# Expert outputs left in PSUM over all steps, x normalised in place, and gathers issued before the turns

## What is computed

```python
x = x + g1[:, None, :] * (merged @ w_out[i])
h = modulate(rms_norm(x, norm2_g[i]), sh2, sc2)
x = x + g2[:, None, :] * grouped_moe(h, router_w, router_bias, moe_w1[i], moe_w3[i], moe_w2[i])

# grouped_moe, t = the 256 tokens; gates = 0 for all but the 2 experts of a token
for e in range(N_EXPERTS):                       # 16 experts
    a = jax.nn.silu(t @ w1[e]) * (t @ w3[e])     # 1024 -> 512
    y = y + gates[:, e:e + 1] * (a @ w2[e])      # 512 -> 1024
```

## Time and profile before

| what | value |
|---|---|
| median of 3 runs | 1086.69 us (1086.66 to 1086.99) |
| profiled execution, span from first to last instruction | 1085.1 us |
| what lies around the span, against the median | 1.6 us |
| PE busy | 1046.2 us (96%), PEld 574.4, DVE 469.5, ACT 174.3 |
| HBM read | 330.54 MB, 306 GB/s over the span |
| chain that ended last | PE 82%, DMA 7%, DVE 6% |
| experts of layer 0, from gather(0) to the end of scatter(6) | 344.1 to 562.3 us |
| experts of layer 1, the same | 857.8 to 1073.4 us |
| PE busy between them, 562 to 857 us | 293.0 of 295 us |
| additions of scattered outputs to x (L1983) | 56, 688 ns each |
| TensorE's mean granted clock | 0.993 |

### The profile page before, as it was taken

How to read it: one execution, slowest core, us unless ns; L and a number is a source line. 1 busy time by engine, 2 the same in 40 slices (tenths; PEclk the granted TensorE clock), 3 DMA queues, 4 the chain that set the end, 5 groups by cost and what they waited for, 6 DMA issues and landing times.

```text
span 1085.1 us, 17591 instructions
## 1 busy us (share of the span) xinstructions
PE 1046.2 (96%) x7533; PEld 574.4 (53%) x7533; DVE 469.5 (43%) x1024; ACT 174.3 (16%) x340; POOL 20.4 (2%) x40
## 2 busy tenths in 40 slices
PE   7999999999999999999999999999999999999885
PEld 3688667654446344443448866765444634444322
DVE  3477696644125422352235769660112532222114
ACT  4021101310014113101121110031001410111102
POOL 3000000000000000000000000000000000000000
PEclk9999999999999999999999999999999999999998
DMA  9997846268953999999999884525665399999992
GB/s 305 391 386 256 304 157 214 79 216 321 413 229 135 411 420 415 421 421 420 421 398 368 295 301 166 185 89 194 252 266 217 137 422 421 420 421 421 421 420 118
DMA packets 90917, 332.78 MB, mean 307 GB/s; under 512 B 5020, under 2 KB 5355, under 8 KB 66005
## 3 DMA queue, kind: packets, MB, share of 16 engines
q1 hardware_dynamic: 87905, 323.56, 76.3%
q0 software_dynamic: 2048, 6.09, 1.6%
q10 hardware_dynamic: 884, 1.97, 0.6%
HBM read 330.54 MB, written 1.05 MB: 306 GB/s over the span
## 4 chain that ended last, share of the span: by engine, by line
PE 82%; DMA 7%; DVE 6%; SPq 3%; issue 1%; ACT 1%; DVEq 0%
PE bank L735 80%; DMA ring<-in_moe_w_dram 3%; SPq L665 2%; DMA wide<-in_moe_w_dram 2%; DMA ring<-in_w_ada_dram 2%; PE bank L1007 1%; PE bank L1175 1%; DVE wide L1586 0%; DVE area L1779 0%; DVE wide L1784 0%; DVE area L1782 0%; PE bank L1093 0%; DVE area L1781 0%; DVE area L1780 0%; PE bank L788 0%
## 5 line engine op out<-in xcount | busy, mean ns | idle before, releaser
L735 PE MATMUL bank<-ring,hT 128*32 128x512 f32 (+3 forms) x1808 | 311.6, 555 | 4.4 <-DMA ring<-in_moe_w_dram 1.8
L735 PE MATMUL bank<-hT,ring 128*32 128x256 f32 (+1 forms) x2112 | 214.1, 380 | 0.2 <-DVE hT L1620 0.2
L735 PEld LDWEIGHTS bank<-ring,hT 128*32 128x32 f32 (+2 forms) x1808 | 129.0, 136 | 152.8 <-issue 149.1
L735 PEld LDWEIGHTS bank<-hT,ring 128*32 128x32 f32 (+1 forms) x2112 | 158.7, 132 | 55.3 <-issue 8.7
L735 PE MATMUL bank<-area 32*64 32x64 f32 (+5 forms) x648 | 96.1, 363 | 0.5 <-ACT area L1468 0.5
L735 PE MATMUL bank<-ring,area 128*32 128x512 f32 x664 | 81.8, 594 | 0.5 <-ACT area L1468 0.5
L2051 DVE TENSOR_TENSOR area<-bank,area 128x512 f32<-128x512 f32 x14 | 9.7, 691 | 148.4 <-PE bank L735 148.4
L735 PEld LDWEIGHTS bank<-area 32*64 32x64 f32 (+4 forms) x648 | 43.8, 145 | 54.2 <-issue 52.2
L735 PE MATMUL bank<-wide,hT 128*32 128x512 f32 x368 | 65.9, 603 | 2.8 <-DMA ring<-in_moe_w_dram 1.4
L735 PE MATMUL bank<-ring,wide 128*128 128x512 f32 (+1 forms) x192 | 64.0, 597 | 0.8 <-DMA ring<-in_w_ada_dram 0.8
L1586 DVE SCALAR_TENSOR_TENSOR area<-ring,wide,area 128x512 f32<-128x512 f32 x84 | 63.1, 751 | 2.5
(11 more groups left out here) (266 smaller groups left out, 895.3 us busy)
## 6 DMA issues: line engine op xcount, KB each, us to landing
ring<-in_moe_w_dram SPq DMA_DIRECT2D x135, 1024.0 KB, 14.5
ring<-in_w_in_dram SPq DMA_DIRECT2D x26, 2048.0 KB, 11.4
ring<-in_w_ada_dram SPq DMA_DIRECT2D x24, 2048.0 KB, 14.2
wide<-in_moe_w_dram SPq DMA_DIRECT2D x33, 1024.0 KB, 12.2
cst<-in_moe_w_dram SPq DMA_DIRECT2D x13, 1024.0 KB, 14.9
area<-in_moe_w_dram SPq DMA_DIRECT2D x11, 1024.0 KB, 14.5
ring<-in_w_out_dram SPq DMA_DIRECT2D x4, 2048.0 KB, 8.0
ring<-in_w_br_h_dram SPq DMA_DIRECT2D x4, 1536.0 KB, 7.9
```

The costliest lines, as they stand in the source:

```text
L735: return pe.matmul(dst, lhsT, rhs, start=start, stop=stop, skip_group_check=True)
```

## The change

- The scattered outputs of all seven steps are summed in banks 2 to 5: only the first step's products start a sum. VectorE adds each bank to x once, after the last step (`add_experts`).
- x is normalised in place: x = x * rs. `root_x` holds the root of the mean square, so that `add_experts` writes x * root_x + bank, which gives the old x back.
- The gather reads x directly, with a step of 8 elements (`chunk_of`), since x isn't regrouped. It writes banks 6 and 7, as banks 2 to 5 are taken, and so does every filter piece.
- xn's memory is a further place for blocks, `NORMED`, free once the output product has read mT (`p_wo`).
- `gather(s + 1)` stands before the turn, with the filter pieces of spot 1 ahead of it; `scatter(s - 1)` stands between the two halves of the turn, and in the last step before `up(6, 1)`. `down(s)` waits until hg has been made from banks 6 and 7.

```diff
@@ place_blocks, SP
-                            + [f for f in free if f[0] < EXTRA] + [(EXTRA + 3, None)]
+                            + [f for f in free if f[0] < EXTRA] + [(NORMED, None), (EXTRA + 3, None)]
...
-            return bank[(5, 4 if L else 7)[n]]
+            return bank[(6 if L else 5, 7)[n]]
...
+                    elif u == NORMED:
+                        sp.wait_ge(p_wo, (L + 1) * 4)
@@ TensorE
+                def chunk_of(tt, k):
+                    return x[:, tt, :].rearrange("p (m k) -> p k m", k=ND)[:, k, :]
 
                 def gather(s):
                     pe.wait_ge(v_sel, L * STEPS + s + 1)
-                    if s >= 2:
-                        pe.wait_ge(v_acc, (L * STEPS + s - 2) * 4 + 2)
+                    if s:
+                        pe.wait_ge(v_yS, (L * STEPS + s - 1) * 2)
+                    if L + 1 < DEPTH and s == TAPS_STEP:
+                        pe.wait_ge(a_dec, (L + 2) * 8)
+                    if L + 1 < DEPTH and s - 1 == TAPS_STEP:
+                        pe.wait_ge(v_kt, (L + 1) * 12 + 8)
+                    if L + 1 < DEPTH and s - 1 == SPECTRA_STEP:
+                        pe.wait_ge(a_ks, (L + 2) * 8)
...
-                            last = mm(bank[2 + k // 4][:, (k % 4) * P:(k % 4 + 1) * P], xn[:, tt, k * P:(k + 1) * P],
+                            last = mm(bank[6 + k // 4][:, (k % 4) * P:(k % 4 + 1) * P], chunk_of(tt, k),
                                       sel[:, tt, :], tt == 0, tt == NT - 1)
...
                 def down(s):
                     n = L * STEPS + s
                     pe.wait_ge(a_actT, n + 1)
+                    if s < STEPS - 1:
+                        pe.wait_ge(a_hg, n + 2)
+                        pe.wait_ge(v_hg, n + 2)
...
                             mm(bank[2 + 2 * tt + h][:, :], selT[:, tt * P:(tt + 1) * P],
-                               yS[:, h * W:(h + 1) * W], True, True).then_inc(p_sc, 1)
+                               yS[:, h * W:(h + 1) * W], s == 0, s == STEPS - 1).then_inc(p_sc, 1)
...
                     up(s, 0)
                     next_filter(s, 0)
+                    if s == STEPS - 1:
+                        scatter(s - 1)
                     up(s, 1)
-                    if s:
-                        scatter(s - 1)
-                    turn(s)
+                    next_filter(s, 1)
                     if s < STEPS - 1:
                         gather(s + 1)
-                    next_filter(s, 1)
+                    turn_act(s)
+                    if 0 < s < STEPS - 1:
+                        scatter(s - 1)
+                    turn_sel(s)
                     down(s)
@@ ScalarE
-                    last = sc.activation(xn[:, tt, :].rearrange("p (k m) -> p k m", k=ND),
-                                         x[:, tt, :].rearrange("p (m k) -> p k m", k=ND), ACT.Copy,
-                                         scale=rs[:, tt:tt + 1])
+                    last = sc.activation(x[:, tt, :], x[:, tt, :], ACT.Copy, scale=rs[:, tt:tt + 1])
...
+                    for u in spectra_in(L, s, 1):
+                        spectrum_kept(u, L + 1)
+                    if s < STEPS - 1:
+                        sc.wait_ge(p_hg, n * 2 + 3)
+                        rows_to_h().then_inc(a_hg, 1)
                     sc.wait_ge(p_actT, n + 1)
@@ VectorE
-                            dv.tensor_tensor(x[:, tt, cols], x[:, tt, cols], bank[2 + 2 * tt + h][:, :], ALU.add)\
-                              .then_inc(v_acc, 1)
+                            dv.wait_ge(p_sc, (L + 1) * STEPS * 4 - 3 + 2 * tt + h)
+                            dv.scalar_tensor_tensor(x[:, tt, cols], x[:, tt, cols], root_x[:, tt:tt + 1],
+                                                    bank[2 + 2 * tt + h][:, :], ALU.mult, ALU.add).then_inc(v_acc, 1)
...
-                    if s:
-                        accumulate(s - 1)
+                    for u in taps_in(L, s, 1):
+                        decayed(u, L + 1)
                     if s < STEPS - 1:
                         dv.wait_ge(p_hg, n * 2 + 4)
                         rows_to_h().then_inc(v_hg, 1)
-                    for u in taps_in(L, s, 1):
-                        decayed(u, L + 1)
```

More of the change, by code:

```diff
@@ L247, in trunk_kernel @@
         sse = sb("sse", [P, NT])
+        root_x = sb("root_x", [P, NT])
         stat = sb("stat", [P, 12, 32])
@@ L257, in trunk_kernel @@
         area = sb("area", [P, AREA])
-        halves += [area[:, AREA - 4 * W:AREA], wide[:, LATE:LATE + 4 * W]]
+        halves += [area[:, AREA - 4 * W:AREA], wide[:, LATE:LATE + 4 * W], xn[:, :, :].rearrange("p t d -> p (t d)")]
         cut = [0]
@@ L377, in trunk_kernel @@
         mask = cst[:, C_MASK:C_MASK + NT * KEYS].rearrange("p (t n) -> p t n", t=NT)
-        slot_in = [sem(f"slot_in{u}") for u in range(ROWS + 1)]
+        slot_in = [sem(f"slot_in{u}") for u in range(NORMED + 1)]
         p_ada = sem("p_ada")
@@ L1169, in up, with turn_act @@
                     last.then_inc(p_up, 1)
-                def turn(s):
+                def turn_act(s):
                     n = L * STEPS + s
@@ L1176, in turn, with turn_sel @@
                     last.then_inc(p_actT, 1)
+                def turn_sel(s):
                     for tt in range(NT):
@@ L1263, in _ @@
                             for tt in range(NT):
-                                last = mm(bank[2 + k // 4][:, (k % 4) * P:(k % 4 + 1) * P],
-                                          xn[:, tt, k * P:(k + 1) * P], sel[:, tt, :], tt == 0, tt == NT - 1)
+                                last = mm(bank[6 + k // 4][:, (k % 4) * P:(k % 4 + 1) * P],
+                                          chunk_of(tt, k), sel[:, tt, :], tt == 0, tt == NT - 1)
                         last.then_inc(X["x_hg"], 1)
@@ L1274, in _ @@
                                 last.then_inc(X["x_up"], 1)
-                        for tt in range(NT):
-                            pe.transpose(bank[4][:, tt * P:(tt + 1) * P], selg[0][:, tt, :], ident)
                         pe.wait_ge(X["x_act"], i + 1)
                         for f in range(NF):
-                            last = pe.transpose(bank[5][:, f * P:(f + 1) * P], act[:, f::NF], ident)
+                            pe.transpose(bank[0][:, f * P:(f + 1) * P], act[:, f::NF], ident)
+                        for tt in range(NT):
+                            last = pe.transpose(bank[1][:, tt * P:(tt + 1) * P], selg[0][:, tt, :], ident)
                         last.then_inc(X["x_turn"], 1)
@@ L1452, in rows_to_h @@
                     for k in range(4):
-                        last = sc.activation(hg[:, k, :], bank[2][:, k * P:(k + 1) * P], ACT.Identity,
+                        last = sc.activation(hg[:, k, :], bank[6][:, k * P:(k + 1) * P], ACT.Identity,
                                              bias=modT[:, 3 * ND + k:3 * ND + k + 1], scale=A2[:, k:k + 1])
@@ L1471, in _ @@
                     sc.activation(selT, bank[1][:, 0:SEQ], ACT.Copy).then_inc(a_selT, 1)
-                    if s < STEPS - 1:
-                        sc.wait_ge(p_hg, n * 2 + 3)
-                        rows_to_h().then_inc(a_hg, 1)
-                    for u in spectra_in(L, s, 1):
-                        spectrum_kept(u, L + 1)
                 sc.wait_ge(v_over, L + 1)
@@ L1485, in _ @@
                     half_k, half_f = ND // 2, NF // 2
-                    sc.wait_ge(v_acc, (L + 1) * STEPS * 4)
+                    sc.wait_ge(p_sc, (L + 1) * STEPS * 4)
                     settle(sc)
@@ L1894, in _ @@
                 dv.wait_ge(a_sq, L * 2 + 2)
-                dv.tensor_tensor(ss[:, :], ssq[:, 1, :], sse[:, :], ALU.add)
+                dv.tensor_tensor(root_x[:, :], ssq[:, 1, :], sse[:, :], ALU.add)
                 link(dv.reciprocal(rs[:, :], rs[:, :]))
-                link(dv.scalar_tensor_tensor(ss[:, :], ss[:, :], -0.5, rs[:, :], ALU.mult, ALU.mult))
+                link(dv.scalar_tensor_tensor(ss[:, :], root_x[:, :], -0.5, rs[:, :], ALU.mult, ALU.mult))
                 link(dv.tensor_tensor(ss[:, :], ss[:, :], rs[:, :], ALU.mult))
@@ L1968, in rows_to_h, with add_experts @@
                     for k in range(4, ND):
-                        last = dv.tensor_scalar(hg[:, k, :], bank[3][:, (k - 4) * P:(k - 3) * P], A2[:, k:k + 1],
+                        last = dv.tensor_scalar(hg[:, k, :], bank[7][:, (k - 4) * P:(k - 3) * P], A2[:, k:k + 1],
                                                 modT[:, 3 * ND + k:3 * ND + k + 1], ALU.mult, ALU.add)
                     return last
-                def accumulate(s):
-                    n = L * STEPS + s
-                    k = 0
+                def add_experts():
                     for tt in range(NT):
@@ L1993, in _ @@
                 dv.wait_ge(p_pos, L * 2 + 2)
-                link(dv.tensor_copy(cnt, bank[6][:, 0:NE]))
+                link(dv.tensor_copy(cnt, bank[4][:, 0:NE]))
                 def inner(a):
@@ L2097, in _ @@
                             dv.wait_ge(X["x_sc"], i + 1)
```

(8 more changed lines are left out.)

40 lines of the change are left out of this document (13 added, 27 removed).

## The result

The changed kernel takes **1132.99 us** (median of 4 runs, 1132.81 to 1133.09) against 1086.84 us for the kernel before beside it: a ratio of 1.042, 95% interval 1.041 to 1.043. The forecast of 1081.6 us was wrong in sign; the rival "strided weights slow the gather" came true at 2.7 times its price per gather (4.1 us, where it took 1.5).

A forecast was written before the change was run, and what follows sets the result against it. Layer 0's expert stage was taken as bound by TensorE with a little help from DMA, layer 1's by DMA plus a tail. Terms of -0.7 and -4.45 us gave 1081.6 us; forecast case 1079.8 to 1083.2, full range 1079.2 to 1086.2.

The forecast's parts named there:

- strided weights slow the gather: Rival: seven gathers per layer slow down by 1.5 us each, giving 1096 us; chance 11 in 100.
- Weights with a stride: The gather's 16 products load weights from x at a step of 8 elements; extra time taken as 0.
- One more place: xn's memory takes one more block in the pause before each expert stage, so later blocks land 2.49 us earlier.
- The transfer was hidden anyway: Rival: the block stream does not end earlier, so layer 1 loses 2.49 us, giving 1084.1 us; chance 12 in 100.
- Waits for blocks in layer 0: TensorE's two waits for blocks in layer 0's last step, 0.52 and 1.32 us, both go: -1.84 us.
- Steps 0 to 5 in layer 0: Gather before the turn, scatter between its halves: step 0 net 0, with the two filter steps together +0.25 us.
- The taps: In layer 0's taps step VectorE no longer reads the gather's banks before the products: saves about 0.4 us.
- The spectra: In layer 0's spectra step the gather now waits for ScalarE's last copy and its signal: 0.65 us more.
- Last step: Scatter of step 5 moves before the second up, uncovering a 0.88 us wait; up's end to down's start 2.19 us, not 4.85.
- Layer 1: Expert stage of layer 1: earlier blocks -2.49, later second up +0.5, shorter tail -2.66, w2 +0.2; sum -4.45 us.
- The wait for w2's second half: Before layer 1's last down, the last block to land is waited for: +0.2 us, between 0 and 0.7.
- The clock: Rival: a fall of TensorE's clock meets layer 1's last up or down, ending 1.4 us later, 1083.0; chance 11 in 100.

The follow-up runs named there:

- d1_forms: Kernel before, each of its 14 gathers replaced by products of another form, width or step; 32 strided two-pass loads took 7.79 us with 32 columns, 14.02 with 512.
- a1_contiguous: Changed kernel, but the gather reads 128 neighbouring features of x per chunk in place of every eighth: 1083.78 us, ratio 0.997 to the kernel before.
- a2_copy_kept: Changed kernel with the regrouped copy xn kept and gathered from, a plain addition at the end and no extra block place: 1086.52 us, ratio 0.999.
- e1_pairs: Changed kernel with the experts' weights laid out by pairs of features: gather at step 2, w1 and w3 read in 4 KB runs: 1089.98 us.
- c1_x_place: Changed kernel, but the regrouped copy xn is kept and gathered from, and x's memory takes the extra block: 1085.61 us, ratio 0.999.
- e2_rows: Changed kernel with the experts' weights laid out so the gather reads neighbours, w1 and w3 read in 2 KB runs: 1102.57 us.

## Why the prediction was wrong, point by point

- **Weights with a stride, taken at 0: this step failed.** I bounded it by 47 ns per load from the mean durations and by 0 from the pace of the transpositions, and chose the pace "because the gather is paced in the same way". It is not: it issues two passes per product, and d1_forms shows 0.24 us per strided load there against 0.12 in a transposition. Measured, the term is 4.1 us per gather and 49.2 us in all. Both bounds came from a one-pass form, so the true 4.1 us per gather lay outside of them. The rival built on them decided from 0.75 us per gather; it had the place right and the price, 1.5 us, wrong. The Trainium skill's rule on lines of 16 bytes spoke against the change, and I outvoted it with the one form here that doesn't follow it.
- **One more place, -2.49: right.** a1_contiguous against a2_copy_kept gives 2.4, and the pause took the block. "The transfer was hidden anyway" is refuted by the same pair.
- **Waits for blocks in layer 0, -1.84: right.** Neither is left in a1_contiguous.
- **Steps 0 to 5 in layer 0.** Step 0 net 0: right, 0.04 in a1_contiguous (a wait of 0.92 before down for the 0.88 before the turn). The taps, taken at -0.4, cost +0.87: the gather now writes the banks that VectorE still multiplies by the decay, a wait of 0.81 with nothing over it, and the inner one of 0.43 stayed. The spectra, +0.65, cost +0.92. In steps 1, 2 and 4 nothing waits: right.
- **Last step.** In layer 0 -0.96 forecast, -0.94 in a1_contiguous. The whole of layer 0 ends 0.7 us later there, not earlier: 0.04 + 0.87 + 0.92 - 0.94 = +0.89, less 0.20 by which its first gather started earlier.
- **Layer 1, -4.45: too much by 1.4.** In a1_contiguous its last scatter starts at 1067.30 for 1069.68, and layer 0 had cost 0.68, so the layer gained 3.1. Counted from the layer's first gather, the second half of w1 in step 6 starts only 2.1 us earlier (1042.81 for 1044.25) and not 2.49. The place alone is worth 2.5 there too (a2_copy_kept starts it at 1048.78, its first gather at 861.93); why the new order takes 0.4 of it back, no run here shows. Up's end to down's start is 2.3 us, forecast 2.19. The wait for w2's second half was taken at 0.2 and is 0.69. I counted four blocks of 2.49 us each to that landing, but the stream thins out at its end: in a1_contiguous it moves 416 GB/s over 1054 to 1058 us, 303 over the next four and 33 over the four behind them. I also left out the longest wait of this layer, 2.71 us at 1011.95, which the trace of before shows ahead of those I listed. In a1_contiguous 0.19 is left in its place, and the next one, listed with 2.13, is 4.17; together 4.84 and 4.36.
- **The clock.** Forecast as a fall that moves near the end of layer 1. There it moved with its wait and cost the same as before, 1.7 us. The one that mattered was new, in layer 0 behind the taps.
- **Order against stride.** Without the stride the forecast would have missed by 2.2 us (1083.78 for 1081.6), still inside its range. By the profiles the two layers miss by 1.4 us each; by the medians beside each other the gain is 3.5 us where 5.1 were forecast. That it is less than the sum of the two is the spread of the runs, no merit of the forecast.
- **The range.** The lower bound of the forecast case, 1079.8, doesn't follow from its terms: 0.5 for the filters, 0.5 for the landings and 0.2 for w2 give 1080.4. The other sums hold.

## What to carry to other kernels

Before a copy that only regroups is removed, price the reader that will see the stride, in the very form that it has: here the time of a gather with two-pass fp32 loads about doubled from a step of 4 values on and hardly changed at a step of 2, although one-pass transpositions of the same shape showed nothing. A load hides beside a product that lasts longer, so the same stride would have cost nearly nothing with 512 moving columns. And try the parts of a large change alone: one moved scatter gave 2.7 us, and the rest needed the waits that it opened to be filled before it paid, and the copy's memory could be had in the buffer that it was copied from.

## What the runs showed of the hardware that was not expected

- Gathers of 32 two-pass weight loads take 3.7 to 3.9 us at steps of 1 and 2 fp32 values, 5.76 at 3, and 7.15 to 8.75 from 4 on. There the time doesn't grow with the step: 16 is the shortest, 12 the longest.
- The time of the strided loads doesn't seem to follow TensorE's clock: after the taps in the changed kernel the granted clock is 0.69 over 474 to 478 us, and that gather lasts 7.87 us like the others at 1.00. In d1_forms the strided gather with 32 columns lasts 7.79 us at a mean clock of 0.74 over 880 to 884 us and 0.50 over 884 to 888. With neighbouring weights a fall shows: in a2_copy_kept (0.50 and 0.71 over 454 to 462 us) it costs the gather 2.9 us, in e1_pairs (0.57 over 454 to 458) 1.5.
- Waits of 0.43 and 0.81 us, with small products of 64 rows between them, are followed by a lower clock in the profiles of the changed kernel, a2_copy_kept and e1_pairs, and not in those of a1_contiguous, c1_x_place and e2_rows, which have the same waits.
- With w1 and w3 in runs of 8, 4 and 2 KB and w2 always in 8, the same queue moved 421, 413 and 397 GB/s.
- At its end a stream of blocks thins out over some 4 us (303 GB/s, then 33, after 416). In a1_contiguous the last eight blocks take 20.9 us (1042.81 to 1063.73), where eight of 2.49 are 19.9.
